# Moving the softmax probabilities: 10 transfers a head from SyncE and 6 from ScalarE, a later place for the products with V, and another order at the end of the attention

## The reference

```python
s = jnp.einsum('bthd,bshd->bhts', qb, kb).astype(F32) * scale + bias
s = jnp.where(valid, s, -jnp.inf)
p = jax.nn.softmax(s, axis=-1).astype(vb.dtype)
return jnp.einsum('bhts,bshd->bthd', p, vb)
...
y_att = o_att @ w_branch_attn
merged = g[:, :, 0] * y_gla + g[:, :, 1] * y_ssm + g[:, :, 2] * y_att
return merged.astype(u.dtype) @ w_out
```

## Time and profile before

| | |
|---|---|
| median of 3 runs | 1780.17 us (1779.62 to 1781.02) |
| the profiled execution | 1782.07 us |
| its span, first to last instruction | 1780.3 us |
| TensorE busy | 1761.9 us (99%) |
| VectorE, ScalarE busy | 975.0 us, 631.1 us |
| granted TensorE clock over the span | 0.999 |
| the attention, from the first scores to the last product with V | about 1039 to 1223 us |

### The profile page before, as it was taken

One profiled execution on the slowest core, in us unless ns is written; L12 is line 12 of the kernel. 1 busy time (PEld: TensorE's weight loads), 2 busy tenths in 40 slices (PEclk: granted clock), 3 DMA queues, 4 the chain that ended last, 5 costly groups with the idle time before them and its releaser, 6 DMA issues.

```text
span 1780.3 us, 26422 instructions
## 1 busy us (share of the span) xinstructions
PE 1761.9 (99%) x9828; PEld 1481.3 (83%) x9828; DVE 975.0 (55%) x1389; ACT 631.1 (35%) x1000; POOL 107.2 (6%) x99
## 2 busy tenths in 40 slices
PE   9999999999999999999999999999999999999998
PEld 7888888888888888888988888887888888888887
DVE  6444443369998988623544556674334544444333
ACT  5222222244455555422333334443223332232221
POOL 2111100000011111000000000000000011111000
PEclk9999999999999999999999999999999999999999
DMA  5322333323333433232223347674222332332332
GB/s 173 105 94 94 98 103 106 106 95 97 96 95 108 100 106 97 86 107 94 95 83 84 112 107 162 145 163 113 95 95 94 95 95 95 98 101 94 106 106 72
DMA packets 162740, 185.59 MB, mean 104 GB/s; under 512 B 111552, under 2 KB 122560, under 8 KB 162672
## 3 DMA queue, kind: packets, MB, share of 16 engines
q1 hardware_dynamic: 111616, 170.18, 31.3%
q10 hardware_dynamic: 51056, 14.50, 4.8%
HBM read 166.21 MB, written 2.16 MB: 95 GB/s over the span
## 4 chain that ended last, share of the span: by engine, by line
PE 89%; ACTq 5%; ACT 2%; DVE 2%; issue 1%; DMA 1%; SPq 1%; DVEq 0%
PE G L650 51%; PE I L650 16%; PE G L717 11%; ACTq L1686 4%; PE G L670 2%; ACT WH L1238 1%; ACT PR L1675 1%; PE G L975 1%; PE I L912 1%; PE I L777 1%; PE I L921 1%; DVE PR L2442 1%; SPq L485 1%; PE I L898 0%; PE I L1087 0%
## 5 line engine op out<-in xcount | busy, mean ns | idle before, releaser
L1790 DVE TENSOR_TENSOR WL<-RAW,WH 128x1024 fp32r<-128x1024 f32 x296 | 375.0, 1270 | 297.2 <-ACT WH L1238 288.4
L1238 ACT CAST WH<-RAW 128x1024 fp32r<-128x1024 f32 x295 | 306.2, 1046 | 232.8 <-PE I L650 126.7
L650 PE MATMUL G<-UH,WH 128*128 128x512 f32 x664 | 164.2, 389 | 0.0
L650 PE MATMUL G<-UL,WH 128*128 128x512 f32 x664 | 164.0, 389 | 0.0
L650 PE MATMUL G<-UH,WL 128*128 128x512 f32 x664 | 164.0, 389 | 0.0
L650 PEld LDWEIGHTS G<-UH,WL 128*128 128x128 f32 x664 | 124.6, 188 | 25.9
L650 PEld LDWEIGHTS G<-UL,WH 128*128 128x128 f32 x664 | 124.6, 188 | 25.9
L650 PEld LDWEIGHTS G<-UH,WH 128*128 128x128 f32 x664 | 124.5, 188 | 25.8
L650 PE MATMUL G<-NH,WH 128*128 128x512 f32 x448 | 114.9, 399 | 3.2 <-ACT ut L1444 3.2
L650 PE MATMUL G<-NL,WH 128*128 128x512 f32 x448 | 111.1, 390 | 0.0
L650 PE MATMUL G<-NH,WL 128*128 128x512 f32 x448 | 110.6, 389 | 0.0
(11 more groups left out here) (351 smaller groups left out, 2594.6 us busy)
## 6 DMA issues: line engine op xcount, KB each, us to landing
RAW<-in_slabs SPq DMA_DIRECT2D x296, 512.0 KB, 3.5
PB<-PR SPq DMA_DIRECT2D x128, 40.0 KB, 2.6
PB<-PR ACTq DMA_DIRECT2D x128, 40.0 KB, 2.7
cum_rows<-kept_rows ACTq DMA_DIRECT2D x16, 256.0 KB, 7.1
y_rows<-y_turned SPq DMA_DIRECT2D x112, 32.0 KB, 3.1
GU<-GO SPq DMA_DIRECT2D x64, 32.0 KB, 1.9
bias<-in_rel ACTq DMA_DIRECT2D x16, 128.0 KB, 4.3
bias<-in_rel ACTq DMA_DIRECT2D x16, 112.0 KB, 2.9
```

The source lines that it names most:

```text
L650: ins = mm(dst, slab(W, n)[:, (k - k0) * P:(k - k0 + 1) * P], R[:, k, :], start=begin and which == 0 and k == k0, stop=end and which == 2 ...
L1238: nc.scalar.copy(slab(WH, n), RAW[:, n.slot, :]).then_inc(split_hi, 1)
L1790: V.tensor_tensor(slab(WL, n), RAW[:, n.slot, :], slab(WH, n).bitcast(F32), ALU.subtract).then_inc(split_lo, 1)
```

## The change

Three edits, with no change in what is computed.

```diff
@@ SyncE, move_probs
-                for b in (0, 1):
-                    for s in range(4):
-                        into, source = probs_piece(e, b, s)
-                        sp.dma_start(into, source).then_inc(probs_moved[e], 16)
+                for k in range(ACT_PIECES, 16):
+                    into, source = probs_piece(e, k // 4, k % 4)
+                    sp.dma_start(into, source).then_inc(probs_moved[e], 16)
@@ ScalarE, move_probs
-                for b in (2, 3):
-                    for s in range(4):
-                        into, source = probs_piece(e, b, s)
-                        act.dma_start(into, source).then_inc(probs_moved[e], 16)
+                for k in range(ACT_PIECES):
+                    into, source = probs_piece(e, k // 4, k % 4)
+                    act.dma_start(into, source).then_inc(probs_moved[e], 16)
@@ TensorE, in every pair (q, f)
-                    att_pieces(q + 1, k, k + 6)
+                    att_pieces(q + 1, k, k + 9)
                     if (q, f) != (0, 0):
                         pe.wait_ge(sems["att_scored"], 16 * (q + 1) + 8 * f + 4)
                         att_pv(*((q, 0) if f else (q - 1, 1)))
-                    att_pieces(q + 1, k + 6, k + 18)
+                    att_pieces(q + 1, k + 9, k + 18)
@@ TensorE, after the last att_pv
-            output_part(n + 1, wn + 1, 0, KT - 1, AH, AL, True, False)
+            output_part(n + 1, wn + 1, 0, 3, AH, AL, True, False)
             pe.wait_ge(sems["att_lo"], last("att_lo", NQ - 1))
             output_part(n, wn, KT - 1, KT, AH, AL, False, True, KT - 1)
-            output_part(n + 1, wn + 1, KT - 1, KT, AH, AL, False, True, KT - 1)
+            output_part(n + 1, wn + 1, 3, KT, AH, AL, False, True, 3)
@@ ScalarE, at the end of the attention
+            merge2_part(*MERGE2_HEAD[5], At(N_MERGE2 + 5), At(W_MERGE2 + 5), False)
             merge2_part(*MERGE2_HEAD[6], At(N_MERGE2 + 6), None)
-            merge2_part(*MERGE2_HEAD[5], At(N_MERGE2 + 5), At(W_MERGE2 + 5), False)
             merge2_part(*MERGE2_HEAD[7], At(N_MERGE2 + 7), None)
@@
+ACT_PIECES = 6
```

## The result

The changed kernel takes 1805.9 us (median of 4 runs, 1799.8 to 1806.3) against 1780.6 us; the ratio is 1.0133, 95% interval 1.0121 to 1.0145. I had forecast 1795 in a range of 1783 to 1808, slower with 0.79. The profiled execution went from 1782.07 to 1805.72 us, +23.65 where the sum said +15.1.

What follows compares the result with a forecast made beforehand. TensorE, busy 1761.9 of 1780.3 us, bounds the kernel, beside a ring of score, turn and transfers. Last products +18.3, tanh wait -3.15, clock -1.7 and +1.7 make +15.1 us: 1795.3, range 1783 to 1808.

Steps and rivals of the forecast that it cites:

- The ring: Attention loop: score of e = 1, `WL`, products with V, burst take 25.1 or 24.6 us a pair against TensorE's 21.64; 0.74.
- the 17.5 of its sum: Burst's first issue to next score of e = 1: today's mean plus 2.65 us, if all hold-ups stay.
- I let it cost the same 1.7 us there: Last products with V: the 3.5 us wait ahead of them costs 1.7 us by a lower clock.
- the upper bound: Whole kernel: bursts of 17.5 us and a clock fall behind each of six loop waits, +28 us, 1808.
- the 24 to 25.5 us named as the sign: Attention loop: distances from pair to pair that the new profile would show; near 22 us would be wrong.
- The row with the 0.76: End of attention, kernel before: granted clock 0.76 over 7 us after the 3.15 us wait, which cost 1.7 us.
- The end: End of attention: the 3.15 us wait for the tanh goes, and 1.7 us of slow clock behind it.
- Landings stay: Rival, transfers: landings stay where they are, only the products' earlier due time counts; +3 us, 1783; chance 0.13.
- Relief wins: Rival, loop: ScalarE's 2.65 us less issuing moves scores up and `WL` is in time; -8.7 us, 1771.5; chance 0.09.
- it pays nothing if the landing holds that score anyway: Loop: ScalarE's relief, score of e = 1 from 1112.34 to some 1110.4, gains nothing from the second pair on.

Runs made afterwards that it cites:

- e6_wl_first: Changed kernel with VectorE's `WL` moved ahead of the score of e = 1 in both pairs: 1779.3 us, 0.9991 of the kernel before.
- e5_filler: Changed kernel with 57 useless matmuls ahead of the six loop waits for `WL`: 1796.0 us, 1.0086 of the kernel before.
- e1_end_only: Kernel before with only the two edits at the end of the attention: 1776.4 us.
- e2_split_only: Kernel before with only the transfers split 10 on SyncE and 6 on ScalarE a head: 1787.3 us.
- e9_later_wl: Kernel before with both end edits, three `WL` moved into VectorE's idle time, products with V after 9 parts, transfers 8 and 8: 1783.5 us, 1.0010.
- e8_after_wl: Changed kernel with all three `WL` of a group moved into VectorE's idle time: 1774.5 us, 0.9962 of the kernel before.
- e4_old_end: Changed kernel with its end of the attention put back, split and later products kept; the end edits give 2.5 us against it.
- e7_end_wl: Kernel before with both end edits and three `WL` moved into VectorE's idle time, transfers 8 and 8: 1773.5 us, 0.9956.

## Why the prediction was right, and where it was not

**The ring: right.** The forecast had 20 us of waits for `WL` "in all" and 3.5 ahead of the last products; the trace has 21.0 and 3.2. It had all scores of e = 1 waiting for transfers, SyncE waiting for the products, ten issues in 6.6 us, and no wait for the tanh; all are there. It said 16.9 us from a burst's first issue to the next score of e = 1; the six in the loop measure 15.8, 16.9, 16.6, 17.3, 16.4 and 17.3 (as 1182.64 to 1199.01), 16.7 in the mean. Why they stay under the 17.5 of its sum, which it put down to a queue behind the slab load, no run shows. e6_wl_first shows that it is a ring and that it runs through `WL`, which the traces of before and after alone could not.

**The mis-sized term: the clock.** The step that failed is "I let it cost the same 1.7 us there", one fall, with falls behind the waits in the loop left to the upper bound. There were six places, five in the loop and one at the last products. Scores of e = 1 and the last products, forecast and measured:

```
            q1f0    q1f1    q2f0    q2f1    q3f0    q3f1    last products
forecast  1093.2  1118.3  1142.9  1168.0  1192.6  1217.7    1238.9
measured  1093.42 1118.94 1145.17 1172.63 1199.01 1227.45   1247.70
```

The first two agree within 0.7 us, the first of them by luck: its burst began 1.3 us later than forecast (1077.60 against 1076.3, behind the slow stretch at 1071) and took 1.1 us less. From there each round is 1.6 to 3.3 us longer than forecast, outside the 24 to 25.5 us named as the sign, and in each of the four a slow stretch begins (1122, 1149, 1177 and, the long one, 1201). From the end of the wait to the end of the products with V it takes 6.4 us in pairs with f = 1, where e5_filler takes 4.9 (1120.52 to 1125.39), and 6.8 and 7.8 us with f = 0, where the undisturbed one takes 5.25 (1096.63 to 1101.88). So a fall costs 1.5 us, and the one at 1201 2.5: some 7 of the 9 us by which the four rounds exceed the forecast. The other 2 I did not track down. TensorE's waits came out at +14.9 us, its busy time at +9.7, together 24.6 for a span that grew by 23.7; the forecast was +15.1 for both. e5_filler, which keeps TensorE at work in the waits, gives 8 to 10 us back. The row with the 0.76 was the evidence for a fall behind a wait of 3.15 us; the forecast waits were as long, six of them, and the consistent reading was to charge each. That would have given +15.1 + 6 x 1.7 = 25.3, 1.7 above what was measured, though only five of the six fell. The upper bound did charge each; its terms, 15.1 + 4 + 10.2, make +29.3 and not the +28 that stands there.

**The end: right in the mechanism.** e1_end_only gives 4.1 us (interval 2.3 to 5.9) for the forecast 4.85: the tanh's wait and the slow stretch behind it went. With the late last products the stretch came back there, as forecast, and the end gives 2.5, which the intervals do not tell from nothing.

**The rivals.** *Landings stay* rested on hold-ups of the queue; e2_split_only (+6.9 us) refutes it. The Trainium skill's "DMA: Bandwidth & Descriptors", section "Issuing engines are not separate DMA queues", calls the sequencer's time usually small; here 4 issues of 0.66 us a pair are what e2 pays for, so the trace does not bear "small" out, though transfers behind a slab load do land late together on both queues (3.7 to 3.9 us after issue at 1136 us in the changed kernel). *Relief wins* was wrong for this kernel, but its mechanism exists: I dismissed `AKL`'s 5.06 us with "it pays nothing if the landing holds that score anyway". e9_later_wl against e8_after_wl shows 9 us hanging on it once the other path is cleared.

## What to carry to other kernels

Before an instruction is moved past another on the busiest engine, ask what that engine will then wait for first and what waits for the instruction moved: the products cost nothing until a wait for a slab stood ahead of them, and then they closed a ring over three engines and a queue. A loss of waits is to be charged with the clock behind each of them, here 1.5 to 2.5 us at five of six waits of 2 to 4 us. And a part can be judged only against the other limits of the moment: the same split cost 7 us here and was worth 9 after three weight copies had moved into idle time.

## What the runs showed of the hardware that I had not expected

The length of a wait does not settle whether the clock falls: in the changed kernel it was at 0.50 behind a wait of 2.16 us and at 1.00 behind one of 2.63, in e4_old_end it stayed at 1.00 behind one of 3.22 (at 1149 us), and in e7_end_wl two waits of 3.4 us together brought one fall. The scatter of the times goes with it: of the changed kernel's four runs three took 1805.7 to 1806.3 us at a mean granted clock of 0.992 to 0.993, and one 1799.8 at 0.996. Useless matmuls in a wait (1.8 to 2.4 us of them, with up to 1.0 us of waiting left behind them) kept the clock at 1.0 in all six places. What makes the clock fall or stay at a given wait was not tried apart.
